# Reordering the front of a hybrid decoder step: linear-attention masks before four key pairs, value pages requested before the state's output, the second sample's value sums inside the first heads

## What is computed

```
z = rmsnorm(h) @ w_in                      # q, k, v of 8 heads of 64; q, k, v of the linear attention; gates
ya = stick_breaking(q, [past_k, k], [past_v, v])   # prompt: its own 512 keys; sample: 4096 past keys in 32 pages
ob, state = gla_scan(qb, kb, vb, log_a, state)     # gated linear attention, 4 heads, chunks of 64 tokens
h = h + (sig(g_a) * (ya @ up_a) + sig(g_b) * (yb @ up_b)) @ w_o
h = h + peer(rmsnorm(h))                   # 8 x 16 experts of 16384 per token, gathered rows
h = h + (p @ w_ple) * sigmoid(rmsnorm(h) @ w_ple_gate)
```

## Time and profile before

| | us |
|---|---|
| median of 3 runs | 2145.82 (2144.64 to 2147.98) |
| the profiled execution's own time | 2150.01 |
| span in its trace | 2148.3 |
| PE busy | 1629.5 (76%) |
| DVE busy | 1366.7 (64%) |
| ACT busy | 658.6 (31%) |
| POOL busy | 790.9 (37%) |
| share of 16 DMA engines' span, queue 0 (issued by POOL) | 74.2% |
| the same, queue 1 (issued by SP) | 16.9% |

### The profile page before, as it was taken

How to read it: one execution, slowest core, us unless ns; L and a number is a source line. 1 busy time by engine, 2 the same in 40 slices (tenths; PEclk the granted TensorE clock), 3 DMA queues, 4 the chain that set the end, 5 groups by cost and what they waited for, 6 DMA issues and landing times. The chain is left out here.

```text
span 2148.3 us, 23990 instructions
## 1 busy us (share of the span) xinstructions
PE 1629.5 (76%) x8044; PEld 749.5 (35%) x8044; DVE 1366.7 (64%) x2673; ACT 658.6 (31%) x1838; POOL 790.9 (37%) x881
## 2 busy tenths in 40 slices
PE   8998978999888757778868677767457557567668
PEld 7647614568345323334422133333012112112112
DVE  1597766877216777665654558778567767575553
ACT  3122214521011333444432333233233433333232
POOL 1232222322253444344434453444334444444440
PEclk9998979999999888898889798899678778878689
DMA  4676696998897999999999999999999999999992
GB/s 163 211 270 208 209 370 221 329 335 301 277 348 293 417 409 418 418 418 419 395 377 421 397 419 420 419 411 419 418 389 405 406 416 400 420 422 388 418 421 106
DMA packets 156875, 769.21 MB, mean 358 GB/s; under 512 B 26440, under 2 KB 26920, under 8 KB 89168
## 3 DMA queue, kind: packets, MB, share of 16 engines
q0 software_dynamic: 103072, 637.59, 74.2%
q1 hardware_dynamic: 53680, 130.10, 16.9%
HBM read 759.41 MB, written 5.58 MB: 356 GB/s over the span
## 5 line engine op out<-in xcount | busy, mean ns | idle before, releaser
L2089 PE MATMUL bank<-arena 64*64 64x512 f32 x4096 | 641.4, 757 | 428.4 <-ACT arena L1153 419.2
L1617 DVE CUSTOM_DVE_ANT_0 arena<-arena 128x1024 f32<-128x1024 f32 x520 | 631.6, 1226 | 484.7 <-DMA arena<-experts_in,arena 477.0
L733 POOL DMA_INDIRECT arena<-experts_in,arena x520 | 600.5, 1155 | 832.5 <-PE bank L2089 709.5
L2089 PEld LDWEIGHTS bank<-arena 64*64 64x64 f32 x4096 | 159.1, 159 | 855.7 <-ACT arena L1153 615.3
L1142 ACT ACTIVATE arena<-arena 128x2 f32<-128x2 f32 x260 | 52.9, 203 | 904.3 <-DVE arena L1617 881.7
L693 POOL DMA_DIRECT2D arena<-cache_k_in x256 | 137.4, 537 | 392.1 <-DVE arena L1215 322.1
L1215 DVE TENSOR_TENSOR arena<-arena 128x1024 f32<-128x1024 f32 x128 | 156.4, 1223 | 28.9 <-DMA arena<-scratch_q 16.6
L1203 DVE TENSOR_REDUCE arena<-arena 128x16 f32<-128x1024 f32 x128 | 155.0, 1214 | 0.0
L1153 ACT ACTIVATE arena<-arena 128x64 f32<-128x64 f32 (+1 forms) x520 | 152.3, 340 | 8.5
L187 ACT ACTIVATE arena<-bank,arena 128x512 f32<-128x512 f32 (+4 forms) x144 | 75.8, 559 | 182.8 <-PE bank L1949 81.9
L187 DVE TENSOR_TENSOR arena<-arena 128x512 f32<-128x512 f32 (+8 forms) x177 | 123.0, 697 | 13.3 <-DMA arena<-xT_in 7.6
(11 more groups left out here) (98 smaller groups left out, 1392.3 us busy)
## 6 DMA issues: line engine op xcount, KB each, us to landing
arena<-cache_k_in POOLq DMA_DIRECT2D x256, 256.0 KB, 4.9
arena<-w_stream_in SPq DMA_DIRECT2D x120, 512.0 KB
arena<-cache_v_in SPq DMA_DIRECT2D x160, 256.0 KB, 5.6
arena<-cache_v_in POOLq DMA_DIRECT2D x96, 256.0 KB, 5.7
arena<-experts_in,arena POOLq DMA_INDIRECT x520
arena<-xT_in SPq DMA_DIRECT2D x4, 520.0 KB, 5.5
arena<-scratch_q SPq DMA_DIRECT2D x1, 2048.0 KB
arena<-x_rows_in SPq DMA_DIRECT2D x2, 1024.0 KB
```

Source lines behind the costliest of these rows:

```text
L733: pool.indirect_dma_start(gring[:, s, :], None, A["experts"], bass.IndirectOffsetOnAxis(ap=rows, axis=0)).then_inc(g_landed[s], 16)
L1617: last = V.tensor_tensor_reduce(gring[:, s, 0:D], gring[:, s, 0:D], x_rows, 1.0, 0.0, ALU.mult, ALU.add, dot[:, s:s + 1])
L2089: last = mm(bank[2 * r + c2][out, :], diag[rows, s], gring[rows, s, cols], start=start, stop=True, skip_group_check=True)
```

## The change

It moves work within the programs of the engines and adds or removes none: each engine has as many instructions as before. VectorE: the masks of the first half come four key pairs earlier (`keys(14)` for `keys(18)`), one pair stands between masks and states instead of three, four pairs follow the states, the state's end is followed by six pairs instead of four, `own_heads(0)` comes ahead of the last two pairs of the normalizations, and the second sample pair's softplus and argument go into head 0. SP: eight value pages are asked for ahead of the state's output, 24 more ahead of the load of `x_rows`. TensorE: sample 1's eight value halves, which stood as one block ahead of the heads, are spread over heads 0 and 1 and what precedes them, and those of samples 2 and 3 follow over heads 1 to 7 as the table `V_IN_HEADS` says. ScalarE follows.

```diff
-FOLD_AT = {0: 1, 4: 2}
-HEAD_KEYS = (5, 5, 5, 5, 4, 4, 4, 4)
+FOLD_AT = {2: 1, 5: 2}
+V_IN_HEADS = (((1, 4), (1, 5)), ((1, 6), (1, 7)), ((2, 0), (2, 1), (2, 2)), ((2, 3), (2, 4), (2, 5)), ((2, 6), (2, 7)),
+              ((3, 0), (3, 1), (3, 2)), ((3, 3), (3, 4), (3, 5)), ((3, 6), (3, 7)))
+HEAD_KEYS = (5, 5, 5, 5, 5, 5, 4, 4)
...
             stream(FRONT_USES, FRONT_USES + RING_W)
+            early_pages(2 * RING_V, 3 * RING_V)
             sp.wait_ge(ss_ready, 1)
             sp.dma_start(A["gla_sample"], sstate).then_inc(out_done, 16)
+            early_pages(3 * RING_V, 6 * RING_V)
             sp.wait_ge(so_ready, 2)
             sp.dma_start(h1A, A["x_rows"][0:2 * P].rearrange("(t p) c -> p t c", p=P)).then_inc(rows_landed, 16)
-            early_pages(2 * RING_V, 4 * PAGES + RING_V)
+            early_pages(6 * RING_V, 4 * PAGES + RING_V)
...
             ob_root(3)
-            take_v(0)
...
-            sample_logs(1)
             act.wait_ge(yb_ready, GH)
             act.wait_ge(out_done, 16 * 5)
             head_logits(0)
-            sample_weights(1)
+            take_v(0)
             head_logs(0)
             head_logits(1)
+            sample_logs(1)
             head_logs(1)
             for h in range(H):
                 head_weights(h)
-                if h in FOLD_AT:
+                if h == 0:
+                    sample_weights(1)
+                elif h in FOLD_AT:
                     take_v(FOLD_AT[h])
...
-            keys(18)
+            keys(14)
...
             gla_masks(0)
-            keys(3)
+            keys(1)
             gla_states(0)
+            keys(4)
             scores_bias(0)
...
             dve.sem_inc(ss_ready, 1)
-            keys(4)
+            keys(6)
...
             for h in range(GH):
                 ob_norm(h)
+                if h == GH - 1:
+                    own_heads(0)
                 keys(2)
-            own_heads(0)
             keys(1)
             scores_bias(1)
-            keys(1)
-            scores_softplus(1)
-            keys(1)
-            own_heads(1)
-            scores_argument(1)
...
                 c.also(V.tensor_tensor, soft, logits, soft, ALU.add, signal=att_sp)
-                if h == 4:
-                    own_heads(2)
-                keys(HEAD_KEYS[h] - 1)
+                if h == 0:
+                    scores_softplus(1)
+                    keys(1)
+                    scores_argument(1)
+                elif h in FOLD_AT:
+                    own_heads(FOLD_AT[h])
+                keys(HEAD_KEYS[h] - (2 if h == 0 else 1))
...
             v_half(0, 7)
-            for n in range(8):
-                if n == 2:
-                    v_fold(0)
-                v_half(1, n)
...
             head_scores(0)
+            v_half(1, 0)
+            v_fold(0)
+            v_half(1, 1)
             pe.wait_ge(v_taken, 1)
             head_scores(1)
-            later_keys(1)
+            v_half(1, 2)
             for h in range(H):
                 head_sums(h)
                 if h in FOLD_AT:
                     v_fold(FOLD_AT[h])
                 if h == 0:
+                    later_keys(1)
+                    v_half(1, 3)
                     pe.wait_ge(dec_arg, 2)
                 head_values(h)
-                v_halves(2 + h // 4, 2 * (h % 4), 2 * (h % 4) + 1)
+                v_half(*V_IN_HEADS[h][0])
                 if h + 2 < H:
                     head_scores(h + 2)
-                v_halves(2 + h // 4, 2 * (h % 4) + 1, 2 * (h % 4) + 2)
+                for b, half in V_IN_HEADS[h][1:]:
+                    v_half(b, half)
```

## The result

| | before | change |
|---|---|---|
| median of the runs of one comparison | 2146.9 (2144.64 to 2150.13, 4 runs) | 2120.58 (2114.37 to 2125.48, 4 runs) |
| the same comparison once more | 2149.39 (2144.65 to 2153.52, 11 runs) | 2117.97 (2114.09 to 2122.11, 5 runs) |
| the profiled execution's own time | 2150.01 | 2125.48 |
| span | 2148.3 | 2123.8 |

The ratio is 0.9875, 95% interval 0.985 to 0.99; in the repetition 0.9853, 0.9836 to 0.9871. By the medians the change is 26 to 31 us faster; 23.8 was forecast (2145.8 to 2122).

The account below looks back on a forecast made before the run. DMA transfers from the state's output to the gates were taken to set the end: 457.9 less 433.9 gives 24.0 us, so 2150.0 becomes 2126.0, or 2122 against the median 2145.8; range 2108 to 2136.

Parts of the forecast that it names:

- Place of the bound: Everything gained lies ahead of the first gate matmul at 457.9 us; the 223.5 us behind it stay unchanged.
- Masks: Ahead of the samples' outputs: TensorE's 6.99 us mask wait goes and the clock recovers, 12.5 us, bounds 7 to 13.
- Pages ahead of the state's output: In sample 0: SP asks for pages earlier, no wait of several us; state's output near 254, normalizations end at 282.0.
- Start of the heads: `head_sums(0)` starts at about 297 instead of 346.16, 49 us earlier, as `head_scores(0)` comes first.
- The end by bytes: From 246.4 to the gates: 64.1 MB at share 0.96 take 187.5 us, ending at 433.9, gain 24.0 us.
- Consumers' end: From the heads to the gates: TensorE would end at 416 and VectorE at 421.5, ahead of the DMA engines.
- rival 1: Up to the gates: consumers set the pace, VectorE's chain ends last at 421.5; gain 36 us, 2110; chance 0.13.
- Rival 2: In head 0: TensorE and VectorE wait for each other, rings stay full; share 0.90, gain 11.5, 2134; chance 0.18.
- Rival 3: In the heads: value halves wait 3.2 us each for pages, TensorE ends 25 us later, 2171; chance 0.06.
- Rival 4: Heads begin earlier but the gates don't, same bytes filling the same time; needs share 0.84; no change; chance 0.03.
- The rule on HBM: Up to the gates: about 358 GB/s per core would cap the gates' gain at 33 us; not taken as limit.
- The sum: Whole execution: 24.0 us off, 2150.0 becomes 2126.0; against the median 2145.8 the forecast is 2122.

Follow-up runs that it names:

- more ahead: The changed kernel with value halves moved earlier, three more key pairs and value pages 16 to 23 asked for sooner; ratio 0.9881 against the kernel before.

## Why the prediction came out as it did

- **Place of the bound.** Right as to the stretch. The gates gained, and the stretch behind them kept its length (223.0 against 223.5 forecast).
- **Masks.** Right: no wait, scores of the second half at 182.37 (181.8 forecast, in an execution that runs 0.7 us later at 156.50), clock 1.00 from 172.4 to 194. The samples' outputs came at 247.0 for 246.4. All of the clock came back.
- **Pages ahead of the state's output.** SP's output at 255.01 for 254. The sign named for this part, no wait of several us for pages in sample 0, did not come: two waits of 3.7 us are left. The last normalization ended at 285.0 for 282.0, three microseconds late; VectorE had waited 3.3 us for a key page, which the sum had at nothing (1.7 in the repetition, which ended it at 282.5). Head 0's addition caught up half of it (298.1 for 296.7). The forecast gave this part no gain of its own; 2.6 us at the gates, not visible in the time.
- **Start of the heads.** `head_sums(0)` at 298.1 for 297.
- **The end by bytes.** The right term for the length of the whole stretch, and the one that was mis-sized. Forecast: 64.1 MB, share 0.96, 356 GB/s at share 1, 187.5 us, 433.9. Measured: 64.3 MB, share 0.98, 356 / 0.98 = 363 GB/s at share 1, 180.5 us, 427.5. The share is worth 3.8 us (2% of 187.5), the rate 3.5; the bytes and the start take 1 back. The rate was scaled up from a stretch with a hole in it. The fullest piece, 366 GB/s, would not have done better: 64.1 MB at that rate end at 421.5, 6.0 us too early, where the forecast was 6.4 too late. As a mechanism the term was only half right. It had the DMA engines set the pace from the state's output on; leaving out pages showed that VectorE sets it in heads 1 and 2, and "more ahead" that 5.3 MB fewer in the stretch move the gates by nothing.
- **Consumers' end.** TensorE's 119 us behind `head_sums(0)` were near: without every second page they took 118.4 (295.0 to 413.4), 4.9 of them that one wait for a page. VectorE's 421.5 was too late. Head 1's addition, which I had ending at 318.3, ended at 316.3 in the change (314.78 + 1.48). Without every second page it started at 312.13, and from its end to the gates were 99.8 us, not 103.2. So rival 1 would have given not 2110 but about 2101 or less.
- **Rival 2** (the rings don't fill the engines) fell for the change: 0.98. Its mechanism, VectorE and TensorE waiting for each other in head 0, is what "more ahead" ran into (4.36 and 3.03 us, share 0.78). **Rival 3** (waits in the heads): a half waited (20.3 + 5.4) / 21 = 1.2 us for its pages where 2.0 would have made it slower than before, and about 1 was forecast. **Rival 4** fell with the share.
- **The rule on HBM** (the Trainium skill, DMA: Bandwidth & Descriptors, Where 436 GB/s comes from: about 358 GB/s for a core). Over the whole stretch the change moved 356 GB/s, which could pass for that limit; but pieces of it have 379 and 378 GB/s, and the gathers 398. The measurement decides: it is no limit here. The gain of 30.4 us, under the 33 that the rule would have allowed, does not decide it.
- **The sum.** The gates gained 30.4 us and not 24.0. The median gained 26.3 in one comparison and 31.4 in the other, against 23.7 forecast: 2120.58 and 2117.97 for 2122, inside the range. That the profiled execution came so close to its own forecast (2125.48 for 2126.0) is luck: its gates came 6.4 us earlier than forecast, and its gathers took 6.4 us longer than before.

## What to carry to other kernels

Where no compute engine fills a stretch and the DMA engines nearly do, start plus bytes over rate is a fair estimate of its end (6.4 us off in 187.5 here), and work which the start is moved past brings its bytes along (12.5 us at the start were 9.6 at the end). But a share near 1 does not show that transfers set the pace in each piece: at 1.00 from 300 to 330 leaving out pages won nothing, and behind head 2 it won 11 us. Once the worst hole is closed, a longer wait (9.57 us) or idle DMA engines (0.56) are no promise: test how far away the next bound is by leaving transfers out (14 us here), and look where in the stretch it binds, before moving more work.

## What was not expected

- Value pages of 64 partitions for 128 took a quarter of the stretch's bytes away and left the DMA engines as busy (1.00 at 261 GB/s); the packets of the whole pages beside them took 29 us more over the span.
- Without every second page the stretch from the gates to the gathers is 3 to 4 us shorter as well (219.7 in the change, 219.7 in the kernel before, for 223.0 and 223.5; the other kernels have 221.4 to 224.9). Sample 4's pages, of which every second is left out too, are used there. That this is the reason was not tested.
- The gathers, 1470 us of work in which nothing differed, varied by 6 us between executions: more than several of the edits are worth. Marks in the trace ahead of them told these edits apart where the time did not.
